# The positional queries of the latent heads: rotated halves from four 32-row products on VectorE in place of a permutation matmul on TensorE, and three PSUM banks shared out differently

## The reference: what is computed

```
lat = h @ w_in                       # 768 query latents, 256 key/value latents, 64 positional key columns
q   = rmsnorm(cq)  @ w_q_up          # 8 heads of 128 + 64 columns
kv  = rmsnorm(ckv) @ w_kv_up         # 8 heads of 128 key + 128 value columns
k   = [k_nope | k_pe]                # k_pe shared by the heads
q, k = rmsnorm per head, then rotary on the last 64 columns:
       x1, x2 = halves of 32;  [x1*cos - x2*sin, x2*cos + x1*sin]
o   = softmax(causal(q k^T / sqrt(192))) v
y   = o @ w_out
```

## Time and profile before

| | |
|---|---|
| median of three runs | 2485.29 us |
| the profiled execution: its own time | 2487.22 us |
| its span | 2485.9 us |
| mean granted TensorE clock | 0.996 of 2.4 GHz |
| TensorE (PE) busy | 2453.1 us, 99% |
| VectorE (DVE) busy | 1715.2 us, 69% |
| ScalarE (ACT) busy | 1173.4 us, 47% |
| GpSimd (POOL) busy | 514.0 us, 21% |
| chain that ended last | PE 87%, DVE 7%, ACT 3%, issue 1%, POOL 1% |

### The profile page before, as it was taken

The page is one execution under the profiler, slowest core; times in us unless marked ns, Lnnn a source line. Parts: engine busy times, 40 slices in busy tenths (PEclk is TensorE's granted clock), DMA queues, the critical chain, the costliest instruction groups (busy, mean ns, idle before and its releaser), DMA issues.

```text
span 2485.9 us, 36528 instructions
## 1 busy us (share of the span) xinstructions
PE 2453.1 (99%) x14410; PEld 2155.1 (87%) x14410; DVE 1715.2 (69%) x2771; ACT 1173.4 (47%) x2028; POOL 514.0 (21%) x442
## 2 busy tenths in 40 slices
PE   9999999999999999999999999999999999999999
PEld 7767778888888989898889898989898888899998
DVE  6896655656634867677868677868677666776766
ACT  4485443444422635355635354535354554554543
POOL 4673302222201201002201002010101432201010
PEclk9999999999999999999999999999999999999999
DMA  5211312333232647452646454555542111456663
GB/s 174 79 43 60 94 51 68 102 93 100 83 102 81 157 134 172 134 149 88 157 135 171 135 149 123 149 145 161 143 121 84 49 52 52 131 153 147 159 146 101
DMA packets 110299, 287.57 MB, mean 116 GB/s; under 512 B 12080, under 2 KB 13616, under 8 KB 110128
## 3 DMA queue, kind: packets, MB, share of 16 engines
q1 hardware_dynamic: 88240, 245.37, 31.4%
q0 software_dynamic: 21888, 39.86, 10.2%
HBM read 283.08 MB, written 2.10 MB: 115 GB/s over the span
## 4 chain that ended last, share of the span: by engine, by line
PE 87%; DVE 7%; ACT 3%; issue 1%; POOL 1%; DMA 0%; SPq 0%; ACTq 0%; POOLq 0%; DVEq 0%
PE main L600 11%; PE main L602 10%; PE main L601 10%; PE score L600 6%; PE score L602 6%; PE score L601 6%; PE main L1969 4%; PE main L1968 4%; PE main L1967 4%; PE score L1967 4%; PE score L1969 4%; PE score L1968 4%; PE out L600 2%; PE out L1969 2%; PE out L1968 2%; PE out L1967 2%
## 5 line engine op out<-in xcount | busy, mean ns | idle before, releaser
L551 DVE TENSOR_TENSOR wl<-raw,wh 128x512 fp32r<-128x512 f32 (+2 forms) x507 | 495.0, 981 | 251.2 <-ACT wh L542 246.6
L542 ACT ACTIVATE wh<-raw 128x512 fp32r<-128x512 f32 (+2 forms) x507 | 415.8, 837 | 479.8 <-PE main L602 249.8
L507 POOL DMA_DIRECT2D sum<-in_wts x152 | 132.9, 903 | 954.7 <-DMA sum<-in_wts 943.6
L551 DVE TENSOR_TENSOR wl<-sum,wh 128x512 fp32r<-128x512 f32 x304 | 207.2, 687 | 62.8 <-ACT wh L542 57.1
L600 PE MATMUL main<-hxh,wh 128*128 128x512 f32 x616 | 242.7, 394 | 3.3 <-DVE hxl L764 1.8
L602 PE MATMUL main<-hxh,wl 128*128 128x512 f32 x616 | 240.1, 390 | 0.0
L601 PE MATMUL main<-hxl,wh 128*128 128x512 f32 x616 | 239.8, 389 | 0.0
L542 ACT ACTIVATE wh<-sum 128x512 fp32r<-128x512 f32 x304 | 177.2, 622 | 82.0 <-PE score L602 42.9
L672 POOL TENSOR_TENSOR acc<-acc,sq 128x512 f32<-128x512 f32 (+1 forms) x73 | 103.1, 1412 | 472.4 <-ACT sq L667 468.8
L1967 PE MATMUL score<-th,wh 128*128 128x256 f32 x548 | 155.4, 284 | 0.7 <-ACT kept L2071 0.5
L1969 PE MATMUL score<-th,wl 128*128 128x256 f32 x548 | 155.1, 283 | 0.0
(11 more groups left out here) (517 smaller groups left out, 7099.2 us busy)
## 6 DMA issues: line engine op xcount, KB each, us to landing
raw<-in_wts SPq DMA_DIRECT2D x299, 512.0 KB, 3.6
sum<-in_wts SPq DMA_DIRECT2D x152, 256.0 KB, 2.9
sum<-in_wts POOLq DMA_DIRECT2D x152, 256.0 KB, 5.0
raw<-in_wts SPq DMA_DIRECT2D x80, 256.0 KB, 5.1
raw<-in_wts SPq DMA_DIRECT2D x52, 384.0 KB, 3.0
x<-in_xT SPq DMA_DIRECT2D x4, 512.0 KB, 7.4
out<-x SPq DMA_DIRECT2D x8, 256.0 KB, 2.0
memx<-in_memT SPq DMA_DIRECT2D x1, 1024.0 KB, 9.6
```

Of the source, the lines that this page charges most:

```text
L507: e.dma_start(t[:, :], stored(r + 1, part), accum_op=ALU.add).then_inc(*sig.up(("upper" if which == S3 else "gate") + f"_ended{n}", ("summ ...
L542: e.activation(halves_of(wh, i), src, ACT.Copy).then_inc(*sig.up("weight_high", ("high", i)))
L551: e.tensor_tensor(halves_of(wl, i), src, f(halves_of(wh, i)), ALU.subtract) \
```

## The change

Four things. (1) `turned_tensor` and its two calls go. (2) `turned_vector` becomes four `scalar_tensor_tensor` instructions of 32 rows: rows 32 to 63 of `qpes` times -1 times the sines go to rows 0 to 31 of `qpesin`, rows 0 to 31 times 1 times the sines to rows 32 to 63, and the same for the lower 64 rows. They wait for `qpes` in place of the bank. (3) The banks: `qpe` of the pairs 2, 4, 6 and the first half of their values go from `heldb` to `shortb`, the keys of heads 2, 4, 6 from `shortb` to `heldb`. (4) Without `qpeturn` in the ring, and with those moves, each later use of banks 0 and 1 may fall on the other one of the two. Nothing else moves.

```diff
         def value_bank(h, half):
-            return scoreb if h == 0 else heldb
+            return scoreb if h == 0 else heldb if half else shortb
...
         def keys_bank(h):
-            return outb if h == 1 else shortb
+            return outb if h == 1 else heldb if h and h % 2 == 0 else shortb
...
+        def query_bank(use):
+            return shortb if use[0] == "qpe" and use[1] else heldb
+
         def query_part(e, i, use, first, last):
 
+            ring = query_bank(use)
             if first == 0:
-                _, old = heldb.take(use)
+                _, old = ring.take(use)
...
-        def turned_tensor(e, h):
-            b, old = shortb.take(("qpeturn", h))
-            e.wait_ge(*sig.at(old))
-            e.wait_ge(*sig.at(("qpes", h)))
-            e.matmul(b[:, :], perm[:, 1, :], qpe_turn.of(("qpes", h))[:, :], start=True, stop=True).then_inc(*sig.up("q_turned", ("qpeturn", h)))
-
         def turned_vector(e, h):
             s, old = qsin_turn.take(("qpesin", h))
-            e.wait_ge(*sig.at(("qpeturn", h)))
-            e.wait_ge(*sig.at(old))
-            e.tensor_tensor(s[:, :], shortb.of(("qpeturn", h))[:, :], cs[:, 1, :], ALU.mult).then_inc(*sig.up("q_sin", ("qpesin", h), ("free", ("qpeturn", h))))
+            e.wait_ge(*sig.at(("qpes", h)))
+            e.wait_ge(*sig.at(old))
+            for to in range(4):
+                r, src = slice(32 * to, 32 * to + 32), slice(32 * (to ^ 1), 32 * (to ^ 1) + 32)
+                e.scalar_tensor_tensor(s[r, :], qpe_turn.of(("qpes", h))[src, :], 1.0 if to % 2 else -1.0, cs[src, 1, :], ALU.mult, ALU.mult) \
+                    .then_inc(*sig.up("q_sin", *([("qpesin", h)] if to == 3 else [])))
...
                 key_rows_tensor(e, h)
-                if h % 2 == 0:
-                    turned_tensor(e, h)
...
             turned_sums_tensor(e, 0)
-            turned_tensor(e, 0)
```

More of the change, by code:

```diff
@@ L2710, in query_part @@
                 e.wait_ge(*sig.at(ready))
-                made = mm3(e, heldb.of(use)[:, :], (h[:, k, :], lo[:, k, :]), (sh, sl), k == 0, k == 5)
+                made = mm3(e, ring.of(use)[:, :], (h[:, k, :], lo[:, k, :]), (sh, sl), k == 0, k == 5)
             if last == 6:
@@ L2715, in turned_scalar @@
         def turned_scalar(e, h):
-            b, s, q = heldb.of(("qpe", h)), qpe_turn.take(("qpes", h)), sqs.take(("qpesq", h))
+            b, s, q = query_bank(("qpe", h)).of(("qpe", h)), qpe_turn.take(("qpes", h)), sqs.take(("qpesq", h))
             e.wait_ge(*sig.at(("unit", qpe_unit(h))))
```

## The result

The changed kernel takes 2510.86 us (median of 4 executions, 2499.24 to 2511.46) where the kernel before took 2485.14 beside it: a ratio of 1.0089, 95% interval 1.0078 to 1.0101. It is slower, as forecast, but 18.4 us above the forecast of 2492.5 and 13.4 above the range. The profiled execution took 2510.82 us, its span is 2509.5, and the mean granted TensorE clock is 0.988 (before: 0.996).

A forecast was written before the change was run, and what follows sets the result against it. TensorE was taken as the bound, busy 151.78 of the heads' stage's 154 us. -3.7 - 1.4 + 0.7 + 3.5 + 5.8 + 0.95 + 1.4 = +7.25 us on the median 2485.29 gave 2492.5, range 2484.5 to 2497.5.

The forecast's parts named there:

- Part 1 and 2: On TensorE: the permutation's four places go, -3.7 us; bank waits before qpe of pair 2 and weight loads go, -1.4.
- The 0.5 for the weight loads: TensorE's other five weight-load waits on bank 2 hold 1.5 us; 0.5 of it taken as gained.
- Part 3: New TensorE bank waits: +0.7 us at turn 4 for head 2's keys, +3.5 at turn 28 before the output projection.
- The bound of 2.3: Lower bound of turn 28's wait, if VectorE's weight step of 1.23 us were out of its way.
- Part 4: Four products on VectorE, taking turns with GpSimd: pairs 4 and 6 wait 2.9 us each for bank 7, +5.8.
- The rival without contention: Short VectorE products not contested by GpSimd: pairs 0 and 2 free, pairs 4 and 6 0.95 each; 2486.3 us; chance 0.18.
- Pair 2: VectorE's four products delay line 2919 to 1980.47 instead of 1978.54; TensorE waits, +0.95 us, lower bound 0.
- Pair 0: Products in turns with GpSimd delay line 2841, which the first score needs: +1.4 us, lower bound 0.
- The sum: All gains and new waits of the main case together: +7.25 us, chance 0.55.
- the clock: Rival: TensorE's clock falls in the new waits, one to three times, +1.7 to +5.1, 2494.2 to 2497.6 us; chance 0.20.

The follow-up runs named there:

- e2: The kernel before with only the banks dealt anew, the permutation and its product kept: 2488.90 us, 0.13% slower than before.
- e3: The changed kernel with one ring step more, so that qsum of head 7 is in bank 0 at turn 28: 2492.59 us.
- e7: The changed kernel with GpSimd starting its two key products of heads 2, 4, 6 only after VectorE's four products: 2495.01 us.
- e5: The changed kernel, unaltered, measured again in 5 executions: 2498.52 us.
- e1: The kernel before with only the four VectorE products in place of the permutation, banks dealt as before: 2500.02 us, 0.63% slower than before.
- e4: The changed kernel with the products of pairs 2, 4, 6 in quarter 0, permutation kept for pair 0, keys of head 2 in bank 7: 2486.48 us.
- e10: The changed kernel with qsum of head 7 in bank 0, line 2941 before the four products, GpSimd's key products after them, values' second half earlier: 2488.49 us.
- e8: e4 with the values' second half (line 2643) ahead of the query scales at quarter 3 of even heads: 2480.84 us, ratio 0.9983 to before.

## Why the prediction was wrong

Direction right, size wrong. Step by step:

- **Part 1 and 2, what goes.** The permutation's 3.7 us and the 0.90 before `qpe` of pair 2 were gained. The 0.5 for the weight loads can't be told apart.
- **Part 3, bank waits that come.** Right in place, cause and size: 3.31 for 3.5 at turn 28 (e2 brings it, e3 takes it away), 0.53 for 0.7 at turn 4. The bound of 2.3 was not needed.
- **Part 4, pairs 4 and 6.** Right: 4.78 for 4.81, 2.77 for 2.9. Both halves of the price were measured apart: held behind one another 2.83 (e7; worked 2.9), and 1.95 more for the turns taken with GpSimd, against 2 x (1.70 - 0.72) = 1.96 from the earlier trace rows. The Trainium skill's hold between instructions on different groups of 32 partitions (VectorE: DVE Perf Modes, section on two Vector instructions with no wait between them) agrees with the 2.83, which is 0.71 from start to start on average. The rival without contention (0.18) is out; with GpSimd out of the way its 0.95 came as 0.81.
- **Pair 2.** Mis-sized, 1.59 for 0.95. Most of the difference is a turn with GpSimd that the working did not have: line 2883, which takes 0.16 us in the kernel before (as 2882), took 0.64 in after, until GpSimd's line 2842 had ended.

```profile
1992.19 0.64 DVE L2883 TENSOR_TENSOR qst<-qst 128x1 f32<-128x1 f32 x1
1990.84 1.98 POOL L2842 TENSOR_TENSOR kn<-tmp,kn 128x512 fp32r<-128x512 f32 x1
```

- **Pair 0.** Right, 1.36 for 1.4.
- **The sum.** 7.25 forecast; 12.3 us of new waits less 3.7 and 0.9 are 7.7, and 7.8 by the stage's length.
- **The step that failed: the clock.** I made it a rival at 0.20, "one to three falls, +1.7 to +5.1", with "TensorE is fully busy around them" against it. That argument is false here: in e5 every one of the four waits of 1.59 us and over brought its fall, 1.53 us each, although the engine was busy at once before and behind. The earlier trace rows had shown such a fall behind small sums and the first score at 1947, in a stage that is 98% busy. It should have been the main case: 7.25 + 4 x 1.53 = 13.4 us, about 2498.6, what after took in six of nine executions. The Trainium skill (TensorE: Matmul & The Clock Gate, part 1), which has the clock lowered after idle time, had been named for turns 14, 22 and 28; e5 agrees at all three, after at the last two. Even my rival stopped at three waits, because pair 2's was taken for too short.
- **What no step had: the long fall at 142 us.** It makes the recorded median 2510.86 and not 2498.5, and is the larger part of the miss: about 10.8 of the 18.4 us. It is no part of the structure: after has it in the profiled execution and not in e5's, with the same program; in the other executions only their time and mean clock speak for it (2510.9 and 2511.5 at 0.988 for two of after; 2510.89 at 0.987 in e1, 2501.07 at 0.990 in e2, 2507.09 at 0.988 in e7; of the kernel before 2497.34 and 2499.0 at 0.991 and 0.990, two in some 60). In e1's profile the clock fell at the same place, behind the same 0.69 us, but for an ordinary fall only:

```profile
140.00:144.00 4.00, 3.31 (x13) 0.77 0.39 133
144.00:148.00 4.00, 4.00 (x16) 0.80 0.00 0
```

So this one place was seen with no fall, a short one and a long one. That the change makes the long one likelier, 3 in 9 against 2 in 60, is not excluded, though the three are all among after's first four executions and none among the five of e5. The kernels share the code there; what decides is not shown, and no run was made against it. This stays open.

- **Which wait brings a fall.** 0.38 us brought one three times in e4; up to 0.95 brought none in e10, nor 1.18 in e7. In the profiles of after and of e1 to e7, behind the first score, the waits of 1.59 to 1.74 us brought a fall in two cases of six (in e3 and e5), those of 2.45 us and over in eleven of thirteen; the two without are turn 14 in after and turn 22 in e3. Behind the first score, which waits 1.36 us in after, e1, e3, e5, e7 and e10, the fall was double in the first three and single in the others. That falls follow waits is shown all the same: in the twelve profiles every fall of the stage stands behind the first score or behind one of TensorE's waits, none anywhere else. The longer waits brought it more often, but length does not decide; what does is open as well.

## What to carry to other kernels

Price a new wait of a busy TensorE at its length plus a likely fall of its clock, here 1.5 us each and behind most waits of 2.5 us and over, and count the waits as well as adding them up: in e3 and e8 more came back than the idle time removed. A step moved to another engine costs what stands behind it there in the queue (the freeing of bank 7, `hqn`'s low part) and what takes turns with it; with those of pairs 2, 4 and 6 one quarter earlier and the values first (e8) the stage is 4.5 us shorter than before, where they were put 13 to 14 longer. And when two executions of one program can differ by 11 us, compare stretches of the traces before explaining a median.

## What the runs showed of the hardware

- Four VectorE products of 32x512 from SBUF, each on other rows than the last, take 2.83 us alone and 4.78 with two GpSimd products of 128x512 ready beside them. GpSimd pays too: 1.52 and 1.72 us, where in e7 line 2835, behind them, took 1.28 (the next one, line 2839, 2.09).
- A fall of the granted clock in the heads' stage lasted about 3.4 us and cost 1.53 us between the same two instructions of two executions.
- A VectorE instruction of one column (line 2883) took 0.64 us in place of 0.16 while a GpSimd product of 128x512 was under way.
- Behind an idle time of 0.7 us at 141 us the same program was granted 1.00 in one execution, and 0.50 for 27 us in another; that is 11 to 12 us at the start of the heads' stage.
